# Expert units put into an order worked out on the chip, and a first product moved ahead of half of the row transposes

## The reference

```python
g_idx = jnp.argmax(grp_logits, axis=-1)                    # one of 4 groups
top_v, top_i = lax.top_k(sel, TOP_K_INNER)                 # 2 of its 4 experts
gate = p_g * jax.nn.softmax(top_v, axis=-1)
for e in range(N_EXPERTS):                                 # 16
    y = (jax.nn.silu(xt @ w_gate[e]) * (xt @ w_up[e])) @ w_down[e]
    out = out + combine[:, e:e + 1] * y
```

## Time and profile before

| | us |
|---|---|
| median of 3 runs | 1076.34 (1075.44 to 1076.48) |
| the profiled execution | 1073.71 |
| its span, first to last instruction | 1071.9 |
| TensorE busy | 969.6 (90%) |
| VectorE busy | 641.8 (60%) |
| ScalarE busy | 462.0 (43%) |
| GpSimd busy | 288.8 (27%) |

### The profile page before, as it was taken

The page is one execution under the profiler, slowest core; times in us unless marked ns, Lnnn a source line. Parts: engine busy times, 40 slices in busy tenths (PEclk is TensorE's granted clock), DMA queues, the critical chain, the costliest instruction groups (busy, mean ns, idle before and its releaser), DMA issues.

```text
span 1071.9 us, 15171 instructions
## 1 busy us (share of the span) xinstructions
PE 969.6 (90%) x5109; PEld 781.7 (73%) x5110; DVE 641.8 (60%) x976; ACT 462.0 (43%) x680; POOL 288.8 (27%) x323
## 2 busy tenths in 40 slices
PE   4899999999998899999678899999999999999950
PEld 3598777789997677776566678888887787777740
DVE  5533277773445656656778876555656756766643
ACT  5321344432224222221347665453546544665533
POOL 2200000000000010000136664342436525555444
PEclk9899999999999999999679999999999999999985
DMA  7421111112035421216579998767777968888857
GB/s 265 95 83 58 39 40 40 41 50 79 31 114 176 163 98 61 77 60 236 182 250 311 334 344 268 239 197 268 210 232 224 316 213 272 258 265 259 297 123 308
DMA packets 89563, 192.28 MB, mean 179 GB/s; under 512 B 8469, under 2 KB 29154, under 8 KB 89522
## 3 DMA queue, kind: packets, MB, share of 16 engines
q1 hardware_dynamic: 79298, 160.89, 43.4%
q0 software_dynamic: 10080, 30.32, 11.2%
q10 hardware_dynamic: 144, 0.52, 0.2%
HBM read 159.28 MB, written 31.42 MB: 178 GB/s over the span
## 4 chain that ended last, share of the span: by engine, by line
PE 69%; DVE 13%; issue 7%; ACT 5%; POOL 2%; DMA 2%; POOLq 0%; DVEq 0%; SPq 0%; ACTq 0%
PE PS L1510 18%; PE PS L1512 17%; PE PS L1511 17%; PE PS L1670 4%; PE PS L1777 2%; DVE WL L1398 2%; PE PS L1758 1%; ACT WH L971 1%; DVE WP L542 1%; DVE HL L1455 1%; DVE XL L1450 1%; DVE HB L1463 1%; PE PS L1685 1%; PE PS L1741 1%; PE PS L1642 1%
## 5 line engine op out<-in xcount | busy, mean ns | idle before, releaser
L1398 DVE TENSOR_TENSOR WL<-RAW,WH 128x2048 fp32r<-128x2048 f32 x100 | 227.3, 2286 | 113.5 <-ACT WH L971 113.5
L971 ACT ACTIVATE WH<-RAW 128x2048 fp32r<-128x2048 f32 x100 | 191.8, 1918 | 16.3 <-PE PS L1512 14.8
L1510 PE MATMUL PS<-WH,XH 128*128 128x512 f32 x404 | 167.4, 414 | 6.3 <-DVE WL L1398 3.3
L1512 PE MATMUL PS<-WH,XL 128*128 128x512 f32 x404 | 159.2, 394 | 0.0
L1511 PE MATMUL PS<-WL,XH 128*128 128x512 f32 x404 | 158.5, 392 | 0.0
L741 POOL TENSOR_TENSOR dst<-dst,stat 128x4 f32<-128x4 f32 x8 | 8.1, 1013 | 351.5 <-DVE dst L1350 351.5
L752 POOL TENSOR_TENSOR stat<-stat 128x1 f32<-128x1 f32 x98 | 71.0, 728 | 104.1 <-ACT YB L1025 86.3
L1510 PEld LDWEIGHTS PS<-WH,XH 128*128 128x128 f32 x404 | 76.5, 189 | 27.7 <-issue 14.6
L1512 PEld LDWEIGHTS PS<-WH,XL 128*128 128x128 f32 x404 | 76.4, 189 | 17.3
L1510 PE MATMUL PS<-WH,HH 128*128 128x512 f32 x200 | 79.2, 396 | 8.6 <-DVE HL L1455 8.6
L1511 PEld LDWEIGHTS PS<-WL,XH 128*128 128x128 f32 x404 | 76.7, 190 | 13.4
(11 more groups left out here) (299 smaller groups left out, 1886.8 us busy)
## 6 DMA issues: line engine op xcount, KB each, us to landing
RAW<-in_w_gate_dram SPq DMA_DIRECT2D x35, 1024.0 KB, 8.2
RAW<-in_w_up_dram SPq DMA_DIRECT2D x34, 1024.0 KB, 9.7
RAW<-in_w_down_dram SPq DMA_DIRECT2D x34, 1024.0 KB, 5.0
wraw<-in_w_in_dram SPq DMA_DIRECT2D x22, 512.0 KB, 4.6
XT<-in_x_dram SPq DMA_DIRECT2D x8, 512.0 KB, 9.5
vo_dram<-vo SPq DMA_DIRECT2D x16, 256.0 KB, 2.1
wout<-in_w_out_dram SPq DMA_DIRECT2D x4, 1024.0 KB, 7.9
VM<-vo_dram SPq DMA_DIRECT2D x16, 256.0 KB, 5.8
```

Of the source, the lines that this page charges most:

```text
L971: A(WH[:, d % SPLITS, :], RAW[:, j, :], ACT.Copy).then_inc(s_whi, 1)
L1398: V.tensor_tensor(WLS[d % SPLITS][:, :], RAW[:, TURN[d][1] if d else 0, :], WH[:, d % SPLITS, :].bitcast(fp32), ALU.subtract).then_inc(s_w ...
L1510: mm(bank, ah, bh, start=start, stop=False)
L1512: return mm(bank, al, bh, start=False, stop=stop)
```

## The change

The units get a second table, `tab2`, in which they stand in another order. It is worked out from `tab`'s counts in four steps, each a small product on TensorE and a few instructions on VectorE: `order_values` (per unit: expert, second half or not, column), `order_keys` (a key per unit), `order_places` (the number of smaller keys is the place; a matrix of zeros and ones moves the three values to their places) and `ordered_table`. With n the unit's number from 1 and r the number of two-half units before it, a one-half unit's key is n - r, its rank among its kind, and a two-half unit's is r + 1.5. The first two units keep their places (150 and 50 are taken from their keys), unused entries get 1000 more and stay last.

All engines read `tab2` in the loop; `tab` still gives unit 0, unit 1's first weight piece and its first gather. The second `s_tab` tells that `tab2` is ready: SyncE waits for it before the store of the gate weights, GpSimd before the gathers of them, TensorE before the loop.

Apart from that, TensorE's quarter 0 of unit 0 now stands behind the row groups 0 and 1 alone, and groups 2 and 3 follow it.

```diff
--- before
+++ after
+        tab2 = at("tab2", cst_at + 4 * (CONST["sel"][0] + 3 * COLS), [P, 3 * NU + 1], i32)
...
+        um = tbuf("um", [NU, 16])
+        uv = tbuf("uv", [NU, 3])
+        uw = tbuf("uw", [NU, NU])
+        ur = tbuf("ur", [NU, 3, NU])
...
             sp.wait_ge(s_cmb, 1)
+            sp.wait_ge(s_tab, 2)
             sp.dma_start(comb_dram.rearrange("(t p e) o -> p t (e o)", p=P, e=NE), comb[:, :, :]).then_inc(s_cmbst, 16)
             with sp.Fori(0, MAXU) as u:
                 with sp.If(u < n_units):
-                    e1 = sp.value_load(tab[0:1, bass.ds(u + 1, 1)], min_val=0, max_val=NE - 1)
-                    e2 = sp.value_load(tab[0:1, bass.ds(u + 2, 1)], min_val=0, max_val=NE - 1)
+                    e1 = sp.value_load(tab2[0:1, bass.ds(u + 1, 1)], min_val=0, max_val=NE - 1)
+                    e2 = sp.value_load(tab2[0:1, bass.ds(u + 2, 1)], min_val=0, max_val=NE - 1)
...
             pool.wait_ge(s_tab, 1)
-            gather(1, 1, 1)
+            gather(1, 1, 1, tab)
             gather_half(1, idxcs[1], 1)
             pool.wait_ge(s_ids, 1)
+            pool.wait_ge(s_tab, 2)
             pool.wait_ge(s_cmbst, 16)
             gather_gates(gix)
...
+            q, rank_, a_, b_, key, fixed, pos_ = (um[:, i:i + w] for i, w in
+                                                  ((0, 4), (4, 1), (5, 1), (6, 1), (7, 1), (8, 1), (9, 1)))
+            expert_, second_, column_ = (uv[:, i:i + 1] for i in range(3))
+            number = C("tokid", NU)[:, 0:1]
+
+            def order_values():
+
+                dve.wait_ge(s_cnt, 4)
+                link(V.tensor_copy(q, PS[0:NU, 4, 0:4]))
+                V.tensor_copy(second_, q[:, 1:2]).then_inc(s_uni, 1)
+                link(V.tensor_scalar(expert_, q[:, 0:1], float(NE - 1), None, ALU.min))
+                link(V.scalar_tensor_tensor(column_, q[:, 2:3], -1.0, number, ALU.mult, ALU.add))
+                link(V.scalar_tensor_tensor(column_, expert_, 4.0, column_, ALU.mult, ALU.add))
+                link(V.tensor_scalar(column_, column_, float(COLS // 2), -1.0, ALU.min, ALU.add))
+                link(V.tensor_scalar(fixed, number, -2.5, 0.0, ALU.add, ALU.min))
+                link(V.tensor_scalar(pos_, number, q[:, 3:4], 1000.0, ALU.is_gt, ALU.mult))
+                V.scalar_tensor_tensor(fixed, fixed, 100.0, pos_, ALU.mult, ALU.add)
+
+            def order_keys():
+
+                dve.wait_ge(s_cnt, 5)
+                dve.wait_ge(s_uni, 3)
+                link(V.tensor_copy(rank_, PS[0:NU, 4, 4:5]))
+                V.scalar_tensor_tensor(a_, rank_, -1.0, number, ALU.mult, ALU.add)
+                link(V.scalar_tensor_tensor(b_, rank_, 2.0, number, ALU.mult, ALU.subtract))
+                link(V.scalar_tensor_tensor(b_, b_, 1.5, second_, ALU.add, ALU.mult))
+                link(V.tensor_tensor(key, a_, b_, ALU.add))
+                link(V.tensor_tensor(key, key, fixed, ALU.add))
+                V.tensor_scalar(uw[:, :], C("ident", NU)[:, 0:NU], key, None, ALU.mult).then_inc(s_uni, 1)
+
+            def order_places():
+
+                dve.wait_ge(s_cnt, 6)
+                link(V.tensor_scalar(ur[:, 0, :], PS[0:NU, 4, 8:8 + NU], key, None, ALU.is_lt))
+                link(V.tensor_reduce(pos_, ur[:, 0, :], AX.X, ALU.add))
+                link(V.tensor_scalar(uw[:, :], C("iota", NU)[:, 0:NU], pos_, None, ALU.is_equal))
+                V.tensor_tensor(ur[:, :, :], uw[:, :].unsqueeze(1).to_broadcast([NU, 3, NU]),
+                                uv[:, :].unsqueeze(2).to_broadcast([NU, 3, NU]), ALU.mult).then_inc(s_uni, 1)
+
+            def ordered_table():
+
+                dve.wait_ge(s_cnt, 7)
+                V.tensor_copy(tab2[:, 0:2 * NU], PS[:, 5, 0:2 * NU])
+                V.tensor_copy(tab2[:, 3 * NU:], tab[:, 3 * NU:])
+                V.tensor_scalar(tab2[:, 2 * NU:3 * NU], PS[:, 5, 2 * NU:3 * NU], 2.0, None,
+                                ALU.mult).then_inc(s_tab, 1)
+
+            order_values()
             lo_piece(0, 0)
+            order_keys()
 
             def scatter_rows():
                 link(V.scalar_tensor_tensor(padf[:, :, :], who[:, :, :], 0.0,
...
                 for d in (6, 7, 8, 9):
                     lo_piece(u, d)
 
-            for g in range(4):
-                x_lo(0, g, 0)
+            x_lo(0, 0, 0)
+            x_lo(0, 1, 0)
+            order_places()
             lo_piece(0, 1)
+            x_lo(0, 2, 0)
+            x_lo(0, 3, 0)
+            ordered_table()
             scatter_rows()
             dve.wait_ge(s_ids, 1)
             dve.wait_ge(s_cmbst, 16)
...
             mm(PS[0:NE, 2, 1:2], C("tri", NE)[:, 0:NE], cs[:, 1:2], start=True, stop=True).then_inc(s_cnt, 1)
             pe.wait_ge(s_uni, 2)
             mm(PS[:, 2, 8:8 + 3 * NU + 1], ones[0:NE, :], acu[:, :], start=True, stop=True).then_inc(s_cnt, 1)
+            for i in range(3):
+                mm(PS[0:NU, 4, i:i + 1], acu[:, NU * i:NU * i + NU], ones[0:NE, 0:1], start=True, stop=True)
+            mm(PS[0:NU, 4, 3:4], ones[0:NE, 0:NU], acu[:, 3 * NU:], start=True, stop=True).then_inc(s_cnt, 1)
+            pe.wait_ge(s_uni, 3)
+            mm(PS[0:NU, 4, 4:5], C("tri", NU)[:, 0:NU], uv[:, 1:2], start=True, stop=True).then_inc(s_cnt, 1)
 
             def x_group(g, par):
                 for k in range(2):
...
                     last = tr(PS[:, 7 - hf, P * f:P * f + P], HB[:, hf, P * f:P * f + P], ident)
                 last.then_inc(s_htt, 1)
 
-            def has_second(u):
+            def has_second(u, tab=tab2):
                 return pe.value_load(tab[0:1, bass.ds(u + NU, 1)], min_val=0, max_val=1)
 
             def unit(u, par):
...
                 down(5, 0, 0, 0).then_inc(s_dn1, 1)
                 down(5, 0, 0, 1).then_inc(s_wused, 1)
 
+            pe.wait_ge(s_uni, 4)
+            mm(PS[0:NU, 4, 8:8 + NU], ones[0:NU, 0:NU], uw[:, :], start=True, stop=True).then_inc(s_cnt, 1)
             pe.wait_ge(s_gath[0], 32)
-            for g in range(4):
-                if g >= 2:
-                    pe.wait_ge(s_xl, g - 1)
-                x_group(g, 0)
+            x_group(0, 0)
+            x_group(1, 0)
             pe.wait_ge(s_tab, 1)
             n_units = pe.value_load(tab[0:1, 3 * NU:3 * NU + 1], min_val=NE, max_val=MAXU)
             pe.wait_ge(s_xl, 2)
             pe.wait_ge(s_wlo, 1)
-            with pe.If(has_second(0) > 0):
+            with pe.If(has_second(0, tab) > 0):
                 gate_up(0, 0, 0, 1)
             gate_up(0, 0, 0, 0).then_inc(s_wused, 1)
+            pe.wait_ge(s_uni, 5)
+            mm(PS[:, 5, 0:3 * NU], ones[0:NU, :], ur[:, :, :].rearrange("p a b -> p (a b)"),
+               start=True, stop=True).then_inc(s_cnt, 1)
+            x_group(2, 0)
+            x_group(3, 0)
+            pe.wait_ge(s_tab, 2)
             with pe.Fori(0, MAXU + 1, 2) as u:
                 with pe.If(u < n_units):
                     unit(u, 0)
```

More of the change, by code:

```diff
@@ L762, in scatter_half, with column, gather @@
                     compute_op=ALU.add).then_inc(s_sca, 16)
-            def column(u):
+            def column(u, tab=tab2):
                 return pool.value_load(tab[0:1, bass.ds(u + 2 * NU, 1)], min_val=0, max_val=COLS - 2)
-            def gather(u, n, par):
-                nc.gpsimd.tensor_copy(idxcs[par][:, :], idx[:, bass.ds(column(u), 2)]).then_inc(s_idxc, 1)
+            def gather(u, n, par, tab=tab2):
+                nc.gpsimd.tensor_copy(idxcs[par][:, :], idx[:, bass.ds(column(u, tab), 2)]).then_inc(s_idxc, 1)
                 pool.wait_ge(s_idxc, n)
@@ L794, in unit @@
                 gather(u + 2, 3 * u + 2, par)
-                second = pool.value_load(tab[0:1, bass.ds(u + 2 + NU, 1)], min_val=0, max_val=1)
+                second = pool.value_load(tab2[0:1, bass.ds(u + 2 + NU, 1)], min_val=0, max_val=1)
                 with pool.If(second > 0):
@@ L811, in unit @@
                 settle(43)
-                filled = pool.value_load(tab[0:1, bass.ds(u + NU, 1)], min_val=0, max_val=1)
+                filled = pool.value_load(tab2[0:1, bass.ds(u + NU, 1)], min_val=0, max_val=1)
                 pool.wait_ge(s_ye, 2 * u + 3)
```

## The result

| | before | changed |
|---|---|---|
| median, us (10 runs each) | 1075.48 (1073.87 to 1077.82) | 1080.96 (1076.76 to 1083.48) |
| profiled execution, us | 1073.71 | 1080.77 |
| its span, us | 1071.9 | 1078.9 |
| first down product, us | 566.96 | 575.23 |
| last unit's first down product, us | 1021.53 | 1028.82 |

The ratio is 1.0056, 95% interval 1.0043 to 1.0070: slower by 5.5 us in the medians, by 6.0 us by the ratio. The difference of their spans, 7.0 us, splits into three: the first down product 8.3 us later, the stretch of 15 pieces 1.0 us shorter (453.6 for 454.6), what follows 0.3 us shorter.

The account below looks back on a forecast made before the run. TensorE was taken as the main bound, with 69% of the chain that ended last. From the median 1076.34 us, +6.3 for the third quarter, +1.0 for gate gathers and -0.8 for the order gave 1082.8, range 1080 to 1085.

Parts of the forecast that it names:

- The sum: Whole kernel: third quarter +6.3, gate-weight wait +1.0, new order -0.8, together +6.5 us.
- The order: Loop over units: the new order takes 453.8 us against 454.6 over 15 pieces, a gain of 0.8 us.
- Step 1: Start of unit 0: TensorE's product of the keys holds the row transposes until 542.5 instead of 540.5, cost 2.0 us.
- Step 2: Early first product of unit 0: starts at 546.3 against 545.9, losing 0.4 us instead of gaining 2.
- Step 3: TensorE's wait for the ordered table before the loop: second gate/up quarter at 556.2 instead of 551.0, late by 5.2 us.
- Step 4: SyncE's gate-weight store waits for the table and delays the third quarter's weight remainder: that quarter late by 6.3 us.
- rival 2: TensorE's clock rises later or is lost while idling for the table: +3.7 us, 1086.5; chance 0.15.
- Step 5: GpSimd's gate-weight gathers, behind the store, make VectorE wait 0 to 2.1 us, taken as 1.0.
- Rival 1: One-half units between two-half units lose their waits: five pieces at 27.8 instead of 29.8, total 1072.8; chance 0.07.

Follow-up runs that it names:

- e3: Kernel before with only the early quarter 0 behind row groups 0 and 1, no second table; ratio to before 1.0029, first down product 38.0 us after `idx` (before 34.0).
- e4: Changed kernel with the waits for the second table moved behind the gate-weight store (SyncE) and gathers (GpSimd); ratio to before 1.0058, first down product 42.3 us after `idx`.
- e7: Changed kernel with 18 added TensorE products ahead of its wait for the table; ratio to before 1.0055, first down product 41.6 us after `idx` (changed 42.3).
- e6: Changed kernel with TensorE's unit 0 written out ahead of the loop, reading the first table; ratio to before 1.0061, first down product 42.4 us after `idx`.
- e8: Changed kernel with the edits of e4, e5 and e6 together; ratio to before 1.0038, first down product 38.9 us after `idx`.
- e10: Changed kernel with all four row groups and row remainders ahead of quarter 0, places and table behind them; ratio to before 1.0048, first down product 40.4 us after `idx`.
- e9: e11 with quarter 0 behind all four row groups and the order computed beside it; ratio to before 1.0021, first down product 38.2 us after `idx`.
- e5: Changed kernel with TensorE's small product of the keys behind row groups 0 and 1; ratio to before 1.0060, first down product 41.0 us after `idx`.
- e11: e8 with row lists behind the keys and the gate-weight store ahead of unit 1's first weight load; ratio to before 1.0008, first down product 36.4 us after `idx`.
- e12: Kernel before with row lists behind the first weight remainder and gate-weight store ahead of unit 1's first weight load; ratio 0.9992, first down product 33.5 us after `idx`.

## Why the prediction was right

**The sum** was +6.5 us, by which the median was to be 1082.8; it is 1080.96, +5.5. Of the 1.8 us between the two, 0.9 is that ten runs put the median of the kernel before at 1075.48, where the forecast started from 1076.34. The sign, the range and the reason (making the order costs more than the order gives) held.

**The order**, -0.8: right, and the firmest term, -1.0 in the trace. It used only lengths of pieces that all occurred. (As printed, rounded, they add up to 453.7; 453.8 is the sum of the unrounded rows.)

**Step 1**, 2.0: the transposes start 2.2 us later, at 542.73 (542.5 forecast).

**Step 2**: quarter 0 at 547.05, forecast 546.3. The 0.8 to 1.0 us of register loads behind the second row remainder remained whole, where half was counted. What the step left out is what e3 shows: the early product costs 3.1 us by itself, through the remainder of piece 2, which comes later, and the clock that falls behind it.

**Step 3**, late by 5.2 at quarter 1: the table came at 555.04 (555.3 forecast), but quarter 1 at 557.57, not 556.2. From the table to the product 2.5 us went by, not 0.85: the branch into the loop, two register loads and the waits of the unit, which the 0.84 of the earlier trace rows does not all contain. Late by 6.6.

**Step 4**, the store as what holds quarter 2: wrong. It landed in 2.1 us, the remainder was ready 2.8 us before TensorE took it, and e4 moved nothing. Quarter 2 is late by 8.3 us instead of 6.3: 1.4 more from step 3 and 1.6 from the clock in quarter 1 (by e7), less the 1.1 by which the remainder was to come behind TensorE. The clock was rival 2, given 0.15 and 3.7 us: its mechanism came, in quarter 1 alone and at less than half its price. The rule of "TensorE: Matmul & The Clock Gate" of the Trainium skill (section "HAM oscillation") that waiting between groups of products puts the engine back to half clock agrees with this trace: 1.00 at 554 to 556, 0.50 at 558 to 560, behind 4.3 us without a product. The fixed price of about 2.0 us that the Trainium skill gives a DMA ("DMA: Bandwidth & Descriptors", section "Anatomy of one DMA", there for the path of GpSimd's DMAs) agrees with the store's 2.1, though SyncE issues it; I had taken 2.6.

**Step 5**, 1.0 (0 to 2.1): no wait in the changed kernel's profile, because TensorE was later still; but 1.2 to 2.5 us in e3, e6, e7 and e8. The two errors, a wait too many here and too little time in steps 3 and 4, lay opposite to each other: +6.3 +1.0 stood for 8.3. That the total came this close is partly luck.

**Rival 1** fell: the 5 DSD pieces take 29.8 each. The distance between 7.1 us in the profiled executions and 5.5 in the medians is mostly that the profiled execution of the kernel before lay 1.8 us under its median.

## What to carry to other kernels

Before reordering work, cut the trace into pieces by what stands next to each other and add the new order up: it told within 0.2 us that alternation was worth 1 us, against a table whose making sat on the path. A chain that just meets its user (here gathers landing 0.1 us before they were wanted) is a second bound, so moving a step later can cost even where the first bound has room, and taking the first away can gain nothing (e6). When a step is moved ahead, list what it pushes back on the other engines: here an early product pushed row remainders, lists and gathers, and a wait of 2.1 us that it made cost the clock as well, 3 us in all. Price an idle stretch of TensorE with what the clock does behind it.

## What the runs showed of the hardware that was not expected

- TensorE's clock fell from 1.00 to 0.50 with waits of 4.3 us (changed kernel), 3.6 (e6), 3.0 (e10) and 2.1 (e3), and stayed at 1.00 through one of 2.3 (e8), so the length of the wait alone does not tell. The quarter behind each fall took 1.6 us more, 2.9 in e10. With 18 products in the gap the clock stayed at 1.00 (e7).
- The clock rose at quite different times after the same VectorE instruction: 14 us (e10, during row transposes alone), 17.8 (before), 23.4 (e9).
- From the writing of the table to the first product, through a loop's entry, two register loads and two branches: 2.5 us on an empty TensorE (2.6 in e10).
- The same store of 64 KB landed in 2.1 to 2.2 us alone (changed kernel, e5, e6, e7, e10), in 4.1 to 4.5 while the gather of unit 0's rows was under way (e9, e11, e12), and in 8.1 to 8.8 behind a load of 1 MB (before, e3, e4, e8).
